# Hybrid encoder layer on one core: 160 columns of the input weights loaded behind the first tile, and the keys' latents projected between the transposes of the input

## The chip, the cores and the metric

The kernel runs on one core of a Trainium2 chip. The metric is the device time of one execution in microseconds (us), the median over several runs. Everything is float32. The engines named below are TensorE (PE, with PEld for its weight loads), VectorE (DVE), ScalarE (ACT), GpSimd (POOL) and SyncE (SP), which here only issues transfers.

## The reference

One encoder layer on a sequence of 512 tokens with 1024 features. The part around the change is the norm and the combined input projection, from which three mixers read their slices:

```python
xn = rms_norm(x, norm1_g[l])
proj = xn @ w_in[l]                      # 1024 x 1472
gq, gk, gv, gg, gaf, gab, fu, cq, ckv, kr = jnp.split(proj, split_at, axis=-1)
o_gla = gla_mixer(gq, gk, gv, gg, gaf, gab, ...)
o_fnet = fnet_mixer(fu, fnet_w[l])
o_mla = mla_mixer(cq, ckv, kr, cos, sin, ...)
x = x + jnp.concatenate([o_gla, o_fnet, o_mla], axis=-1) @ w_out[l]
x = x + hier_moe(rms_norm(x, norm2_g[l]), ...)   # 32 experts, top 2
```

`ckv` (128 columns) is the latent from which the attention's keys and values are made, `kr` (32 columns) the rotary part of the keys. They are the last 160 of the 1472 columns of `w_in`.

## The kernel before

The tokens are four tiles of 128 (`T` = 4), the features eight groups of 128 (`C` = 8). Each engine runs its own instruction list in the order in which the code issues it, and semaphores join them. The eight PSUM banks (512 float32 columns each) are given out by `psum_plan`, a list written by hand: `ring` takes the next bank, `open_bank` lets PE wait until the bank's last reader is through, `filled` lets a reader wait for PE, and `drained` lets anyone wait until the readers are through.

The order at the start is this. SP issues the positions, the four tiles of x (0.5 MB each, semaphores `x_landed`), and then `w_in` in three pieces: columns 0 to 255 (q and k of the linear attention, 1 MB), 768 to 1471 (2.8 MB), 256 to 767 (2 MB). PE transposes x (L747), eight 128x128 blocks for each tile of tokens; the block of group c goes to bank c, so a bank is full only when the last tile has been transposed. ACT (even banks) and DVE (odd banks) copy the eight banks into `xnT`, scaled by the first norm's gain, one instruction of 512 columns for each bank (L1283, L1532). ACT also squares x for the norm (L1275, two instructions in the profile for each tile: the square and the read of its sum), two tiles before and two behind its copies. The norm's root is applied to the products, not to x: DVE builds `rdiag` from it (L1538, semaphore `rstd_ready`).

PE's products follow: `pT 1` (L771, q by feature, waits for the first piece of `w_in` and for each copied bank), `R` (L776), `pT 2` (L755), `pT 0` (L781), then for each tile t the product `ckr` (L763, 160 columns: latent and rotary part of the keys) and the product `ucq` (L763, 512 columns), with the two gate products `z` (L792) behind the first tile's, and then four products `vg` (L763, 512 columns). Each product by token is eight matmuls, one for each group of features; a float32 matmul shows as two records in the profile. Behind them come the latents' transposes (L801, L806, wait for `latents_ready`), those of the gated keys (L812, wait for `gla_ready`), and all of the attention, the output projection, the router and the experts.

ACT copies each `ckr` product to SBUF, squares its latent and then squares a part of `ucq` (`copy_ckr`, L1294 to L1299), in turns with the exponentials of the gates. The experts' weights (3 MB for each of 32 experts) stream through seven places in SBUF; SP issues a load when PE is through with the place's last expert (`gu_full`, L631, `y_full`, L636; for the first place that comes free `gu_half`, L677).

Of the kernel before, what the change touches and what calls it, by code (L numbers as in the profile page):

```python
# [30 lines left out]
ALU = mybir.AluOpType  # L31
# [3 lines left out]
P = 128  # L35
# [33 lines left out]
def psum_plan():  # L69
# [12 lines left out]
    def ring(key, readers=1):  # L82
        use(key, turn[0] % 8, readers)
        turn[0] += 1

    for c in range(C):
        ring(("xT", c))
# [4 lines left out]
    for t in range(T):  # L92
        ring(("ckr", t))
        ring(("ucq", t))
        if t == 0:
            ring(("z", 0))
            ring(("z", 1))
# [134 lines left out]
def encoder_kernel(nc, d, out):  # L232
    ctx = ExitStack()
    with ctx:
# [170 lines left out]
        win_landed = [sem(f"win_landed{i}") for i in range(3)]  # L405
# [164 lines left out]
        def _(sp):  # L570
# [3 lines left out]
            for t in range(T):  # L574
                sp.dma_start(X[:, t, :], x_v[:, t, :]).then_inc(x_landed[t], 16)
            sp.dma_start(w_in_sb[:, :, GQ:GV], w_in_v[:, :, GQ:GV]).then_inc(win_landed[1], 16)
            sp.dma_start(w_in_sb[:, :, GA:W_IN], w_in_v[:, :, GA:W_IN]).then_inc(win_landed[0], 16)
# [161 lines left out]
        def _(pe):  # L739

            pe.wait_ge(ident_landed, 16)
            for t in range(T):
                pe.wait_ge(x_landed[t], 16)
                for c in range(C):
                    if t == 0:
                        open_bank(("xT", c))
                    mm = pe.transpose(banks[PLAN[("xT", c)][0]][:, t * P:(t + 1) * P], X[:, t, c:D:C], ident[:, :])  # L747
                    if t == T - 1:
                        close_bank(mm, ("xT", c))
# [16 lines left out]

            pe.wait_ge(win_landed[1], 16)
            ps = open_bank(("pT", 1))
            for c in range(C):
                drained(pe, ("xT", c))  # L770
                mm = pe.matmul(ps[:, :], w_in_sb[:, c, GQ:GQ + 128], xnT[:, c, :], start=(c == 0), stop=(c == C - 1))  # L771
            close_bank(mm, ("pT", 1))
# [11 lines left out]
            for t in range(T):  # L784
                by_token(("ckr", t), t, CKV, 160)
                by_token(("ucq", t), t, FU, 512)
                if t == 0:
                    pe.wait_ge(gate_w_landed, 16 * 8)
                    drained(pe, ("pT", 0))
                    for dd in range(2):  # L790
                        ps = open_bank(("z", dd))
                        close_bank(pe.matmul(ps[:, :], wa[:, dd, :], gaT[:, :], start=True, stop=True), ("z", dd))  # L792
# [463 lines left out]
        def _(act):  # L1256
# [20 lines left out]

            square_x(0)
            square_x(1)
            act.wait_ge(first_landed, 48)  # L1280
            for c in range(0, C, 2):
                ps = filled(act, ("xT", c))
                free_bank(act.activation(xnT[:, c, :], ps[:, :], ACT.Copy, scale=gain1[:, c:c + 1]), ("xT", c))  # L1283
            square_x(2)
            square_x(3)
            root_guess(stat[:, 8:12], stat[:, 4:8])
# [5 lines left out]
            def copy_ckr(t):  # L1292
# [4 lines left out]
                act.wait_ge(squares_ready, T + 2 * t + 1)  # L1297
                drained(act, ("ucq", t))
                act.activation(squares_out, ucq[:, t, 256:512], ACT.Square, accum_out=stat[:, 16 + t:17 + t]).then_inc(squares_ready, 1)  # L1299
                act.wait_ge(squares_ready, T + 2 * t + 2)  # L1300

            act.wait_ge(rstd_ready, T)
            copy_ckr(0)

# [4 lines left out]
            copy_ckr(1)  # L1309
# [5 lines left out]
            copy_ckr(2)  # L1315
            copy_ckr(3)
# [180 lines left out]
        def _(dve):  # L1497
# [32 lines left out]
            for c in range(1, C, 2):  # L1530
                ps = filled(dve, ("xT", c))
                free_bank(dve.tensor_scalar(xnT[:, c, :], ps[:, :], gain1[:, c:c + 1], None, ALU.mult), ("xT", c))  # L1532
# [573 lines left out]
```

## Time and profile before

| | |
|---|---|
| median of 3 runs | 520.05 us (518.36 to 520.24) |
| the profiled execution's own time | 521.45 us |
| its span on the core | 519.6 us |
| PE busy | 488.5 us (94%) |
| DVE, ACT, POOL busy | 213.0, 137.7, 75.5 us |
| HBM read, written | 129.94 MB, 16.39 MB |

The span is the stretch from the first to the last instruction of the profiled execution; 1.85 us of its time lie around it. PE's busy time counts pipelined matmuls with modelled ends. The profile divides the span into 40 slices of 13 us; the DMA engines are busy at 90% or more in the last 20 slices but one, which is the time of the experts.

### The profile page before, as it was taken

To read this page: it belongs to the slowest core of one execution; us is meant where nothing else is said; L and a number is where in the kernel's file an instruction comes from. 1 tells how busy PE (TensorE), PEld (TensorE's weight loads), DVE (VectorE), ACT (ScalarE), POOL (GpSimd) and SP (SyncE) were. 2 spreads that over 40 slices of the span, in tenths; PEclk is the share of its full clock that TensorE was granted. 3 is DMA by queue.
4 is the path that set the end of the run, shared out by engine and by line. 5 is a ranking of instruction groups with operands and counts; after the bars stand their busy time and mean duration, and the time that the engine had idled before them with its cause. 6 is when DMAs were issued, how large, how long until landed. Compare 5 with 4: busy or idle time off the path is not lost.

```text
span 519.6 us, 7646 instructions
## 1 busy us (share of the span) xinstructions
PE 488.5 (94%) x2904; PEld 262.6 (51%) x2904; DVE 213.0 (41%) x562; ACT 137.7 (27%) x359; POOL 75.5 (15%) x101
## 2 busy tenths in 40 slices
PE   4999999999999999999999899999999998879894
PEld 4446544567655554455455555555555554444431
DVE  3217330576776661116853322222222222242167
ACT  4404211354676661213131111111111111112023
POOL 1000000352100000001122122222222222111000
PEclk9999999999999999999999899999999999999998
DMA  8995000010298005941398999999999999999974
GB/s 299 360 276 223 2 1 0 16 37 3 77 420 354 1 1 211 425 173 42 96 334 301 408 373 422 419 419 418 418 419 418 418 418 419 420 419 420 401 289 162
DMA packets 35543, 139.42 MB, mean 268 GB/s; under 512 B 9865, under 2 KB 11977, under 8 KB 23473
## 3 DMA queue, kind: packets, MB, share of 16 engines
q1 hardware_dynamic: 30160, 130.85, 64.3%
q0 software_dynamic: 4816, 7.85, 4.1%
q8 instruction: 24, 0.39, 0.3%
q10 hardware_dynamic: 528, 0.22, 0.2%
q14 instruction: 15, 0.11, 0.1%
HBM read 129.94 MB, written 16.39 MB: 282 GB/s over the span
## 4 chain that ended last, share of the span: by engine, by line
PE 72%; DMA 17%; DVE 6%; SPq 3%; issue 1%; ACT 1%; DVEq 0%; POOLq 0%; ACTq 0%
PE bank L1090 16%; PE bank L763 12%; PE bank L952 9%; PE bank L1103 7%; DMA MIX<-in_moe_w_up 6%; DMA EW<-in_moe_w_up 5%; PE bank L925 4%; PE bank L997 3%; PE bank L986 3%; DMA EW<-y_scratch 2%; PE bank L1062 2%; DMA EW<-in_w_in 2%; SPq L631 2%; PE bank L771 1%; PE bank L869 1%; DMA y_scratch<-G,sidx 1%
## 5 line engine op out<-in xcount | busy, mean ns | idle before, releaser
L1090 PE MATMUL bank<-EW,WO 128*64 128x256 f32 x640 | 78.5, 397 | 6.9 <-DMA EW<-in_moe_w_up 4.2
L763 PE MATMUL bank<-EW,XT 128*128 128x512 f32 (+1 forms) x192 | 64.1, 495 | 0.0
L1090 PEld LDWEIGHTS bank<-EW,WO 128*64 128x64 f32 x640 | 45.0, 137 | 35.1 <-DMA EW<-in_moe_w_up 6.6
L952 PE MATMUL bank<-WO,XT 128*128 128x512 f32 x128 | 56.9, 596 | 0.0
L1444 ACT ACTIVATE G<-bank 128x128 f32<-128x128 f32 x32 | 8.9, 278 | 179.1 <-PE bank L1090 169.5
L1815 DVE TENSOR_TENSOR G<-G,bank 128x128 f32<-128x128 f32 x32 | 9.2, 288 | 107.4 <-ACT G L1444 107.4
L2040 POOL DMA_INDIRECT y_scratch<-G,sidx x30 | 30.5, 1017 | 154.3 <-DVE G L1828 138.9
L763 PEld LDWEIGHTS bank<-EW,XT 128*128 128x128 f32 x192 | 32.9, 190 | 31.0 <-issue 31.0
L1828 DVE COPY G<-bank 128x512 f32<-128x512 f32 x32 | 22.1, 692 | 46.2 <-PE bank L1103 46.2
L1103 PE MATMUL bank<-EW,G 128*64 128x512 f32 x160 | 38.2, 599 | 0.0
L952 PEld LDWEIGHTS bank<-WO,XT 128*128 128x128 f32 x128 | 23.6, 190 | 26.9 <-issue 26.9
L925 PE MATMUL bank<-EW 96*128 96x512 f32 x64 | 32.8, 596 | 0.9 <-ACT WO L1363 0.6
L1680 DVE TENSOR_REDUCE nm<-bank 128x1 f32<-128x512 f32 x32 | 22.0, 689 | 14.3 <-PE bank L925 14.1
L2034 POOL DMA_INDIRECT list_scratch<-lrow,dest x8 | 7.9, 990 | 131.0 <-DVE dest L1772 129.8
L1374 ACT ACTIVATE G<-bank,nm 128x512 f32<-128x512 f32 x32 | 22.0, 688 | 12.0 <-DVE nm L1680 10.0
L986 PEld LDWEIGHTS bank<-ident,G 128*128 128x128 f32 x128 | 15.3, 140 | 14.9 <-issue 13.9
L1434 ACT ACTIVATE WO<-bank,gain 128x128 f32<-128x128 f32 x64 | 18.3, 369 | 14.2 <-PE bank L1062 14.2
L1394 ACT ACTIVATE EW<-bank 128x512 f32<-128x512 f32 x32 | 18.7, 590 | 8.9 <-PE bank L986 8.9
L986 PE MATMUL bank<-ident,G 128*128 128x128 f32 x128 | 19.3, 275 | 0.0
L1103 PEld LDWEIGHTS bank<-EW,G 128*64 128x64 f32 x160 | 10.4, 135 | 15.6 <-issue 13.2
L1090 PE MATMUL bank<-MIX,WO 128*64 128x256 f32 x128 | 15.4, 391 | 2.1 <-DMA MIX<-in_moe_w_up 2.1
L1090 PE MATMUL bank<-XT,WO 128*64 128x256 f32 x128 | 15.4, 391 | 2.0 <-DMA XT<-in_moe_w_up 2.0
(296 smaller groups left out, 623.5 us busy)
## 6 DMA issues: line engine op xcount, KB each, us to landing
EW<-in_moe_w_down SPq DMA_DIRECT2D x20, 1024.0 KB, 22.4
EW<-in_moe_w_gate SPq DMA_DIRECT2D x19, 1024.0 KB
EW<-in_moe_w_up SPq DMA_DIRECT2D x19, 1024.0 KB
y_scratch<-MIX SPq DMA_DIRECT2D x8, 512.0 KB, 8.4
WO<-in_w_out SPq DMA_DIRECT2D x2, 2048.0 KB, 11.7
MIX<-in_moe_w_gate SPq DMA_DIRECT2D x4, 1024.0 KB
MIX<-in_moe_w_up SPq DMA_DIRECT2D x4, 1024.0 KB
G<-in_moe_w_down SPq DMA_DIRECT2D x4, 1024.0 KB
```

The costliest lines, as they stand in the source:

```text
L763: mm = pe.matmul(ps[:, 0:width], xnT[:, c, t * P:(t + 1) * P], w_in_sb[:, c, col:col + width], start=(c == 0), stop=(c == C - 1))
L925: close_bank(pe.matmul(ps[:, :], qT[0:QD, h, tq * P:(tq + 1) * P], kT[0:QD, h, :], start=True, stop=True), ("S", i))
L952: mm = pe.matmul(ps[:, :], xnT[:, c, t * P:(t + 1) * P], w_out_sb[:, c, n * 512:(n + 1) * 512], start=(c == 0), stop=(c == C - 1))
L986: mm = pe.transpose(ps[:, kc * P:(kc + 1) * P], probs[:, i % 4, kc * P:(kc + 1) * P], ident[:, :])
L1090: mm = pe.matmul(bank[BLOCK * m:BLOCK * (m + 1), 0:2 * P].rearrange("p (w n) -> p w n", w=2), xeT[:, c, par * BLOCK:(par + 1) * BLOCK], wv ...
L1103: mm = pe.matmul(bank[BLOCK * q:BLOCK * (q + 1), :], hT[:, par, m, :], wv[:, m, q * 512:(q + 1) * 512], start=(m == 0), stop=(m == 1))
L1374: free_bank(act.activation(probs[:, i % 4], ps[:, :], ACT.Exp, bias=nm[:, i:i + 1], accum_out=rs[:, i:i + 1]), ("S", i))
L1394: free_bank(act.activation(probsT[:, g, u, :, tile * P:(tile + 1) * P], ps[:, :].rearrange("p (k n) -> p k n", k=T), ACT.Copy), ("PT", j))
L1434: ins = act.activation(xeT[:, c], banks[half][:, j * P:(j + 1) * P], ACT.Copy, scale=gain2[:, c:c + 1])
L1680: dve.tensor_reduce(nm[:, i:i + 1], ps[:, :], AX, ALU.max, negate=True).then_inc(neg_max, 1)
L1828: dve.tensor_copy(Y[:, e % 2], banks[4 + e % 2][:, :]).then_inc(y_ready, 1)
L2040: pool.indirect_dma_start(y_rows, bass.IndirectOffsetOnAxis(ap=sidx[:, col:col + 1], axis=0), Y[:, e % 2], None, bounds_check=4 * S - 1, o ...
```

## The change

The last 160 columns of `w_in` become a transfer of their own, issued behind the first tile of x. The transposes go to two banks for each tile (four groups each), so that a tile can be copied as soon as it has been transposed: DVE copies four groups with one instruction of 512 columns, ACT the other four with four instructions of 128 columns. PE makes the four `ckr` products between and behind the transposes. The other products keep their order. ACT copies all four `ckr` before it squares the first `ucq`. The core of the diff:

```diff
-    for c in range(C):
-        ring(("xT", c))
+    for t in range(T):
+        for q in range(2):
+            ring(("xT", t, q))
+    for t in range(T):
+        ring(("ckr", t))
     ring(("pT", 1))
     ring("R")
     ring(("pT", 2))
     ring(("pT", 0))
     for t in range(T):
-        ring(("ckr", t))
         ring(("ucq", t))
...
             for t in range(T):
                 sp.dma_start(X[:, t, :], x_v[:, t, :]).then_inc(x_landed[t], 16)
+                if t == 0:
+                    sp.dma_start(w_in_sb[:, :, CKV:W_IN], w_in_v[:, :, CKV:W_IN]).then_inc(win_landed[3], 16)
             sp.dma_start(w_in_sb[:, :, GQ:GV], w_in_v[:, :, GQ:GV]).then_inc(win_landed[1], 16)
-            sp.dma_start(w_in_sb[:, :, GA:W_IN], w_in_v[:, :, GA:W_IN]).then_inc(win_landed[0], 16)
+            sp.dma_start(w_in_sb[:, :, GA:CKV], w_in_v[:, :, GA:CKV]).then_inc(win_landed[0], 16)
...
+            def transpose_x(t):
                 pe.wait_ge(x_landed[t], 16)
+                for q in range(2):
+                    ps = open_bank(("xT", t, q))
+                    for j in range(4):
+                        mm = pe.transpose(ps[:, j * P:(j + 1) * P], X[:, t, 4 * q + j:D:C], ident[:, :])
+                    close_bank(mm, ("xT", t, q))
...
+            def key_latent(t):
+                for q in range(2):
+                    drained(pe, ("xT", t, q))
+                by_token(("ckr", t), t, CKV, 160)
+
+            transpose_x(0)
+            pe.wait_ge(win_landed[3], 16)
+            key_latent(0)
+            transpose_x(1)
+            transpose_x(2)
+            key_latent(1)
+            transpose_x(3)
+            key_latent(2)
+            key_latent(3)
             pe.wait_ge(win_landed[1], 16)
-            ps = open_bank(("pT", 1))
-            for c in range(C):
-                drained(pe, ("xT", c))
-                mm = pe.matmul(ps[:, :], w_in_sb[:, c, GQ:GQ + 128], xnT[:, c, :], start=(c == 0), stop=(c == C - 1))
-            close_bank(mm, ("pT", 1))
+            by_feature(("pT", 1), GQ, 128)
...
             for t in range(T):
-                by_token(("ckr", t), t, CKV, 160)
                 by_token(("ucq", t), t, FU, 512)
...
+            def copy_x(t):
+                ps = filled(act, ("xT", t, 1))
+                for j in range(4):
+                    ins = act.activation(xnT[:, 4 + j, t * P:(t + 1) * P], ps[:, j * P:(j + 1) * P], ACT.Copy,
+                                         scale=gain1[:, 4 + j:5 + j])
+                free_bank(ins, ("xT", t, 1))
+
             square_x(0)
+            act.wait_ge(first_landed, 48)
+            copy_x(0)
             square_x(1)
-            act.wait_ge(first_landed, 48)
-            for c in range(0, C, 2):
-                ps = filled(act, ("xT", c))
-                free_bank(act.activation(xnT[:, c, :], ps[:, :], ACT.Copy, scale=gain1[:, c:c + 1]), ("xT", c))
             square_x(2)
+            copy_x(1)
+            copy_x(2)
             square_x(3)
+            copy_x(3)
...
             act.wait_ge(rstd_ready, T)
-            copy_ckr(0)
-
+            for t in range(T):
+                copy_ckr(t)
+            square_cq(0)
...
+            def copy_x(t):
+                ps = filled(dve, ("xT", t, 0))
+                free_bank(dve.tensor_tensor(xnT[:, 0:4, t * P:(t + 1) * P], ps[:, :].rearrange("p (c n) -> p c n", c=4),
+                                            gain1[:, 0:4].unsqueeze(2).to_broadcast([P, 4, P]), ALU.mult), ("xT", t, 0))
+
             dve.wait_ge(first_landed, 48)
+            copy_x(0)
             dve.tensor_copy(lrow[:, :, :, 0], small[:, 41:49].rearrange("p (t r) -> p t r", t=T)).then_inc(row_ready, 1)
```

On PE, at the start of the program, the order before was this. L747 are the transposes, L771 the product `pT 1`, which waits for one copied bank after another (`bank_free`) and for its weights (`win_landed1`):

```order
L747 MATMUL bank<-ident,X 128x128 [waits x_landed0,ident_landed]
L747 MATMUL bank<-ident,X 128x128 x7
L747 MATMUL bank<-ident,X 128x128 [waits x_landed1]
L747 MATMUL bank<-ident,X 128x128 x7
L747 MATMUL bank<-ident,X 128x128 [waits x_landed2]
L747 MATMUL bank<-ident,X 128x128 x7
L747 MATMUL bank<-ident,X 128x128 [waits x_landed3]
L747 MATMUL bank<-ident,X 128x128 x7
L771 MATMUL bank<-XT,EW 128x512 [waits bank_free0,win_landed1]
L771 MATMUL bank<-XT,EW 128x512 [waits bank_free1]
```

The same place on PE in the changed kernel, whose line numbers differ: L751 are the transposes, L766 the `ckr` products:

```order
L751 MATMUL bank<-ident,X 128x128 [waits x_landed0,ident_landed]
L751 MATMUL bank<-ident,X 128x128 x7
L766 MATMUL bank<-EW,XT 128x160 [waits bank_free1,bank_free0,win_landed3]
L766 MATMUL bank<-EW,XT 128x160 x7
L751 MATMUL bank<-ident,X 128x128 [waits x_landed1]
L751 MATMUL bank<-ident,X 128x128 x7
L751 MATMUL bank<-ident,X 128x128 [waits x_landed2]
L751 MATMUL bank<-ident,X 128x128 x7
L766 MATMUL bank<-EW,XT 128x160 [waits bank_free1,bank_free3,bank_free2]
L766 MATMUL bank<-EW,XT 128x160 x7
L751 MATMUL bank<-ident,X 128x128 [waits x_landed3]
L751 MATMUL bank<-ident,X 128x128 x7
```

Behind these rows stand the other two `ckr` products and then `pT 1`, so all four are now ahead of it. The first waits for the copies of the first tile, and the transposes of the other tiles stand behind it.

On ACT, at the start of the program, the order before: L1275 squares, L1283 copies, L1268 begins the norm's root:

```order
L1275 ACTIVATE MIX,stat<-X 128x1024 [waits x_landed0]
L1275 ACTIVATE MIX,stat<-X 128x1024 [waits x_landed1,squares_ready]
L1283 ACTIVATE XT<-bank,gain 128x512 [waits bank_full0,first_landed,squares_ready]
L1283 ACTIVATE XT<-bank,gain 128x512 [waits bank_full2]
L1283 ACTIVATE XT<-bank,gain 128x512 [waits bank_full4]
L1283 ACTIVATE XT<-bank,gain 128x512 [waits bank_full6]
L1275 ACTIVATE MIX,stat<-X 128x1024 [waits x_landed2]
L1275 ACTIVATE MIX,stat<-X 128x1024 [waits x_landed3,squares_ready]
L1268 ACTIVATE stat<-stat 128x4 [waits var_ready,squares_ready]
```

And in the changed kernel, where L1287 squares and L1293 copies:

```order
L1287 ACTIVATE MIX,stat<-X 128x1024 [waits x_landed0]
L1293 ACTIVATE XT<-bank,gain 128x128 [waits bank_full1,first_landed,squares_ready]
L1293 ACTIVATE XT<-bank,gain 128x128 x3
L1287 ACTIVATE MIX,stat<-X 128x1024 [waits x_landed1]
L1287 ACTIVATE MIX,stat<-X 128x1024 [waits x_landed2,squares_ready]
L1293 ACTIVATE XT<-bank,gain 128x128 [waits bank_full3,squares_ready]
L1293 ACTIVATE XT<-bank,gain 128x128 x3
L1293 ACTIVATE XT<-bank,gain 128x128 [waits bank_full5]
L1293 ACTIVATE XT<-bank,gain 128x128 x3
L1287 ACTIVATE MIX,stat<-X 128x1024 [waits x_landed3]
L1293 ACTIVATE XT<-bank,gain 128x128 [waits bank_full7,squares_ready]
L1293 ACTIVATE XT<-bank,gain 128x128 x3
```

Four copies of 512 columns have become sixteen of 128, each tile's copies stand behind a square, and the third square stands ahead of the second tile's copies.

## Rows read from the trace of the kernel before

**Rows 1.** PE's waits over the span: us in total, times, longest.

```profile
PE bank L747 <- DMA X<-in_x: 5.5, 1, 5.5
...
PE bank L1090 <- DVE rslot L1848: 1.9, 1, 1.9
...
PE bank L771 <- DMA EW<-in_w_in: 1.7, 1, 1.7
```

**Rows 2.** The chain that ended last: start, us, what.

```profile
3.46 9.26 DMA EW<-in_w_in
12.76 7.13 PE bank L771 x16
...
40.43 54.59 PE bank L763 x160
...
407.79 32.36 DMA MIX<-in_moe_w_up
```

**Rows 3.** SP's queue, 120 to 330 us, in order of time.

```profile
275.96 0.33 SPq L677 DMA_DIRECT2D EW<-in_moe_w_gate  x1
```

**Rows 4.** Busy by stretch: PE, PEld, DVE, ACT, POOL; then clock, DMA share, GB/s.

```profile
5.40:6.90 1.50, 1.41 (x7) 1.45 (x8) 0.25 (x3) 1.12 (x2) 0.00 (x0) 1.00 1.01 385
...
20.00:30.00 10.00, 10.00 (x38) 4.06 (x37) 2.54 (x4) 0.00 (x0) 0.00 (x0) 1.00 1.10 229
...
320.00:400.00 80.00, 80.00 (x565) 41.18 (x563) 23.37 (x51) 10.47 (x37) 19.04 (x19) 1.00 1.02 419
```

**Rows 5.** PE, 0 to 150 us: start, us, line, operation, count, idle before.

```profile
5.49 5.62 PE L747 MATMUL bank<-ident,X 128*128 128x128 f32 x32 [5.49 <-DMA X<-in_x]
...
29.40 9.31 PE L763 MATMUL bank<-EW,XT 128*128 128x160 f32 x32
...
96.25 1.04 PE L812 MATMUL bank<-ident,WO 128*128 128x128 f32 x8
```

**Rows 6.** PE in the window 8.4 to 8.9 us.

```profile
8.08 1.06 PE L747 MATMUL bank<-ident,X 128*128 128x128 f32 x4
```

**Rows 7.** PE in the window 9.93 to 10.7 us.

```profile
9.71 1.17 PE L747 MATMUL bank<-ident,X 128*128 128x128 f32 x9
```

**Rows 8.** Line L747, the transposes of x at the start: ns min/median/max.

```profile
L747 PE MATMUL bank<-ident,X x32: 272/421/451, 5.5 to 10.8; 128*128 128x128 f32 x32
```

**Rows 9.** Line L1019, the same transpose later: ns min/median/max.

```profile
L1019 PE MATMUL bank<-ident,X x32: 272/274/348, 216.1 to 261.4; 128*128 128x128 f32 x32
```

**Rows 10.** By form, 0 to 96 us: busy us, mean ns, idle before.

```profile
L763 PE MATMUL bank<-EW,XT 128*128 128x160 f32 x64 | 9.5, 301 | 0.0
```

**Rows 11.** All engines, 0 to 48 us, in order of time.

```profile
5.37 1.06 ACT L1275 ACTIVATE MIX<-X 128x1024 f32<-128x1024 f32 x1 [1.85 <-DMA X<-in_x]
...
6.34 0.19 ACT L1275 ACTIVATION_READ_ACCUMULATOR MIX<-X 128x1 f32 x1
6.62 0.17 DVE L1515 COPY lrow<-small 128x8 f32<-128x8 f32 x1 [6.62 <-DMA gain<-in_norm_g]
...
7.12 1.06 ACT L1275 ACTIVATE MIX<-X 128x1024 f32<-128x1024 f32 x1 [0.60 <-DMA X<-in_x]
...
17.95 1.28 ACT L1291 ACT_TABLE_LOAD   x1
...
27.66 0.69 DVE L1546 TENSOR_TENSOR G<-bank,MIX 128x512 f32<-128x512 f32 x1 [5.45 <-PE bank L755]
```

**Rows 12.** ACT in the window 286 to 288 us: four copies of 128 columns.

```profile
286.38 1.14 ACT L1434 ACTIVATE WO<-bank,gain 128x128 f32<-128x128 f32 x4 [2.52 <-PE bank L1062]
```

**Rows 13.** DVE, 47 to 96 us: the last instruction of the gates' chain.

```profile
55.43 0.69 DVE L1584 TENSOR_TENSOR WO<-G,dec 128x512 f32<-128x512 f32 x1
```

**Rows 14.** PE in the window 290 to 310 us, around a long wait.

```profile
295.78 5.44 PE L1090 MATMUL bank<-EW,WO 128*64 128x256 f32 x32 [1.89 <-DVE rslot L1848]
```

**Rows 15.** PE there in quarters of a us: busy; granted clock, DMA share, GB/s.

```profile
296.50:296.75 0.25, 0.25 (x4) 0.50 1.24 524
...
299.75:300.00 0.25, 0.25 (x6) 1.00 0.84 295
```

More of the change, by code:

```diff
@@ L404, in encoder_kernel @@
         x_landed = [sem(f"x_landed{t}") for t in range(T)]
-        win_landed = [sem(f"win_landed{i}") for i in range(3)]
+        win_landed = [sem(f"win_landed{i}") for i in range(4)]
         first_landed = sem("first_landed")
@@ L741, in _ @@
             pe.wait_ge(ident_landed, 16)
-            for t in range(T):
+            def transpose_x(t):
                 pe.wait_ge(x_landed[t], 16)
-                for c in range(C):
[L745 to L749, printed above, removed]
+                for q in range(2):
[3 more added lines that the diff above has]
+                    close_bank(mm, ("xT", t, q))
             def by_feature(key, col, width):
@@ L765, in by_token @@
                 close_bank(mm, key)
-            pe.wait_ge(win_landed[1], 16)
-            ps = open_bank(("pT", 1))
-            for c in range(C):
-                drained(pe, ("xT", c))
-                mm = pe.matmul(ps[:, :], w_in_sb[:, c, GQ:GQ + 128], xnT[:, c, :], start=(c == 0), stop=(c == C - 1))
-            close_bank(mm, ("pT", 1))
+            def key_latent(t):
[11 more added lines that the diff above has]
+            key_latent(3)
+            pe.wait_ge(win_landed[1], 16)
+            by_feature(("pT", 1), GQ, 128)
             pe.wait_ge(ones_ready, 1)
@@ L1296, in copy_ckr, with square_cq @@
                 act.activation(squares_out[:, 0:128], ckr[:, t, 0:128], ACT.Square, accum_out=stat[:, 20 + t:21 + t]).then_inc(squares_ready, 1)
-                act.wait_ge(squares_ready, T + 2 * t + 1)
+                act.wait_ge(squares_ready, T + t + 1)
+            def square_cq(t):
                 drained(act, ("ucq", t))
                 act.activation(squares_out, ucq[:, t, 256:512], ACT.Square, accum_out=stat[:, 16 + t:17 + t]).then_inc(squares_ready, 1)
-                act.wait_ge(squares_ready, T + 2 * t + 2)
+                act.wait_ge(squares_ready, 2 * T + t + 1)
             act.wait_ge(rstd_ready, T)
-            copy_ckr(0)
+            for t in range(T):
+                copy_ckr(t)
+            square_cq(0)
             for dd in range(2):
@@ L1308, in _ @@
                 act.activation(gexp[:, dd, 1], gexp[:, dd, 0], ACT.Ln, bias=1.0).then_inc(gate_log, 1)
-            copy_ckr(1)
+            square_cq(1)
             for dd in range(2):
@@ L1314, in _ @@
                 act.activation(dec[:, dd], tot[:, dd], ACT.Exp, scale=1.0 / TAU).then_inc(decay_exp, 1)
-            copy_ckr(2)
-            copy_ckr(3)
+            square_cq(2)
+            square_cq(3)
             root_guess(stat[:, 32:40], stat[:, 24:32])
@@ L1527, in _ @@
             dve.tensor_scalar(kk, kk, float(np.pi / 2), None, ALU.add).then_inc(angles_ready, 1)
-            for c in range(1, C, 2):
-                ps = filled(dve, ("xT", c))
-                free_bank(dve.tensor_scalar(xnT[:, c, :], ps[:, :], gain1[:, c:c + 1], None, ALU.mult), ("xT", c))
+            for t in range(1, T):
+                copy_x(t)
             dve.wait_ge(squares_ready, T)
```

## The prediction

> **What bounds the kernel now.** I read PE's waits first [rows 1]. PE waits 5.5 us for the first tile of x, 1.7 us for the first piece of `w_in`, and then for nothing until the attention, some 130 us in; only short waits follow until the experts. So up to the experts the time is PE's own work. The chain that ended last [rows 2] says the same: from 12.76 us on it runs on PE from product to product, among them one piece of 54.59 us that holds the last `ckr` products. The late part is another matter. From about 320 us the DMA engines move 419 GB/s without a gap [rows 4], and the chain runs through a transfer of experts' weights of 32.36 us [rows 2]. But that stream begins with issues that PE releases: the first place that comes free is reloaded at 275.96 us [rows 3], behind the first expert's first products. What PE gains or loses before that moves the stream and with it the end, one for one. So I ask one question: when does PE begin the product `pT 1`, once the four `ckr` products are counted on one side in both kernels?
>
> **Before.** `pT 1` begins at 12.76 us [rows 2]. The four `ckr` products come later and cost 9.5 us of PE for 64 records [rows 10], 0.148 us a record or 2.37 us a product. With them moved ahead and nothing else, `pT 1` would begin at 12.76 + 9.5 = 22.26 us. That is the number to beat.
>
> **A clock behind the transposes.** The 32 transposes take 5.62 us [rows 5], and not evenly. In one window four take 1.06 us [rows 6]: less the last one's 0.42 us, the median of the line [rows 8], that is 0.64 / 3 = 0.213 us from one to the next. In a later window nine take 1.17 us [rows 7]: (1.17 - 0.27) / 8 = 0.112 us. The same form takes a median 0.274 us later in the kernel against 0.421 us here [rows 8, 9]. [...] The records grant 1.00 at this time [rows 4], so the level is my reading of the spacing. If n transposes ran slow, 0.213n + 0.112(32 - n) = 5.62 - 0.3 gives n = 17: the clock rose about 5.49 + 17 x 0.213 = 9.1 us, taken as 9.3.
>
> **After, step by step.** Removed: PE's wait of 1.66 us for the first piece of `w_in`, which is far behind its landing when `pT 1` comes. Added, in PE's order:
>
> Tile 0 is transposed from 5.49 us at the slow rate: the last of eight starts at 5.49 + 7 x 0.213 = 6.98 and ends at 7.40. DVE copies its half at about 7.0 to 7.7 us: its bank is full at about 6.6, the gain lands at 6.62 [rows 11], and 512 columns from a bank take 0.69 us, as the form with two operands does [rows 11]. ACT has to square tile 0 first, 5.37 to 6.53 [rows 11], which is over before the second bank is full. Then four copies of 128 columns take 1.14 us [rows 12]: 7.45 to 8.6. So the first `ckr` begins at about 8.65, and PE has a new wait of 1.25 us, with all other transposes behind it.
>
> The weights for it: 655 KB behind the first tile. At 385 GB/s [rows 4] that is 1.7 us, landing at 7.1; at the worst rate of the nearest rows, 229 GB/s [rows 4], 2.9 us and 8.3. Both are ahead of 8.65, so the transfer is hidden behind the copies. The other tiles come 1.7 to 2.9 us later than before: tile 1, squared from 7.12 before [rows 11], at 8.8 to 10.0, and the others 1.36 us apart (524 KB at 385 GB/s), tile 3 at 11.5 to 12.7. All are needed later than that. [...]
>
> First `ckr`: slow until 9.3 (0.3 us a record by the factor of two, so two records), the other 14 at 0.148: ends at about 11.35. Transposes of tiles 1 and 2: 16 x 0.112 = 1.8, to 13.15. Second `ckr`: needs ACT's copies of tile 1. Its bank is full at 12.45; ACT's second and third squares (1.25 us each, 8.8 to 11.4) are done; copies to 13.6. A wait of 0.5 us. It ends at 13.65 + 2.37 = 16.0. Tile 3: to 16.9. Third `ckr` (its copies end at 14.8): to 19.3. ACT's last square takes 14.8 to 16.05, its copies of tile 3 17.1 to 18.3, ahead of the last `ckr`: 19.3 to 21.65. `pT 1` begins at about 21.7.
>
> Sum: 22.26 - 21.7 = 0.55 us earlier. By parts: 1.66 us of waiting gone, 1.75 us of waiting new, 15 - 6 = 9 transposes fewer at the slow rate saves 0.9, two slow records of `ckr` cost 0.3. The sum is made on the profiled execution (521.45 us, span 519.6), 1.4 us above the median of the runs; a shift of half a us is the same on both. 520.05 - 0.55 = 519.5.
>
> **Edits costed at nothing.** The norm's root comes later on ACT, behind the last copies at 18.3, with `rdiag` about 2.1 us after them (root, three small steps, four instructions of 0.22), at 20.4. `R` needs it behind `pT 1` (7.13 us [rows 2]), at 28.8: cover of 8 us. ACT's four `ckr` copies follow the table loads (1.28 us each [rows 11]) at about 22, and no bank of theirs is used again before `ucq 0`, at 21.7 + (29.40 - 12.76) = 38.3 us [rows 5, 2]. The gate products `z` come 3 x 2.37 - 0.55 = 6.6 us later than before, since all four `ckr` are ahead of them and not only one, so their chain on DVE ends at about 63 instead of 56; its reader on PE is at 96.25 [rows 13, 5]. The latents' norm stays where it is, since the last `ucq` moves only by the sum above. Nothing behind `ckr` on SP or POOL waits for a thing that moves: SP only issues 1,024 more short rows in a queue that is full of data anyway. Were these covers gone, the largest would cost the 2.1 us of `rdiag`.
>
> **Rivals.** *The clock stays low through the first `ckr`.* The change cuts the run of transposes by a wait of 1.25 us where before PE ran unbroken. This kernel shows what a wait can do: before L1090 PE waits 1.89 us, the granted clock stands at 0.50 as it resumes and is back at 1.00 at 299.75 [rows 15], and 32 records take 5.44 us [rows 14]. Before, the rise came 9.3 - 5.49 = 3.8 us after PE began. If the wait makes that count anew from the first `ckr`, it comes at 8.65 + 3.8 = 12.5: 13 records run slow instead of two, 11 x 0.15 = 1.7 us more than in my sum. Then 520.05 - 0.55 + 1.7 = 521.2, slower than before. It decides from a rise at about 10.4 us on: from there the gain is gone. Against it: the wait is shorter than 1.89 us, and the wait of 1.66 us before `pT 1` left the clock up. [...]
>
> *More is gained.* If the copies are quick and the clock is up by the first `ckr`, 0.3 us more is saved; and if in runs of before that nobody profiled the wait of 1.66 us brought the clock down (some 3.5 us at half rate, as in [rows 14, 15], are 1.7 us lost), the change saves that too: 518.2.
>
> *The shift is swallowed.* If the experts' stream does not hang on PE, nothing moves: 520.05. Against it stands the issue at 275.96, which waits for PE [rows 3].
>
> *The transfer breaks the order.* If the short rows run at a third of the rate (5 us), tile 1 lands at 12, and PE waits another 1.7 us: 521.2 too. No row has such a rate.
>
> **How the numbers follow.** My forecast 519.5, own range 518.8 to 520.1: 0.45. Clock low, or low for part of it, 521.2: 0.25. More gained, 518.2: 0.12. Swallowed, 520.05: 0.1. Slow transfer, 521.2: 0.03. Something that I do not see, either way: 0.05. Half a per cent is 2.6 us, about what a measurement can tell from no change; no case reaches it alone. Two together, clock and transfer, could. The runs also scatter, from 518.36 to 520.24. The range is 518.0 to 521.9. Faster by over 0.5%: 0.07; within: 0.84; slower: 0.09.
>
> **What would show it.** In the profile of the changed kernel: PE idle of 1.0 to 1.5 us ahead of the first `ckr` (released by ACT's copies, not by the DMA); transposes of tiles 1 to 3 at 0.11 us; a short wait ahead of the second `ckr`, released by ACT; `pT 1` at 21.3 to 22.1 us without a wait for weights; no new wait until 96 us; the first L677 issue as much earlier as `pT 1` is against 22.26. I am wrong if the first `ckr` takes over 3 us, if PE waits for `win_landed3` or a tile, or if `pT 1` begins after 22.5.

## The result and the profile after

The changed kernel takes **521.87 us** (median of 11 runs, 520.60 to 523.91) against 520.05 us (518.36 to 521.34, 11 runs): a ratio of 1.0033, with a 95% interval of 1.0018 to 1.0048. It is slower, by a third of a per cent. Forecast was 519.5 us. The range, 518.0 to 521.9, holds the time at its very edge, but the step was in the other direction.

PE's work in order of time, 0 to 320 us (start, us, line, operation, count, idle before and what ended it):

```profile
5.79 1.94 PE L751 MATMUL bank<-ident,X 128*128 128x128 f32 x8 [5.79 <-DMA X<-in_x]
9.26 3.89 PE L766 MATMUL bank<-EW,XT 128*128 128x160 f32 x16 [1.52 <-ACT XT L1293]
12.98 1.94 PE L751 MATMUL bank<-ident,X 128*128 128x128 f32 x16
15.36 2.41 PE L766 MATMUL bank<-EW,XT 128*128 128x160 f32 x16 [0.44 <-issue]
17.61 1.05 PE L751 MATMUL bank<-ident,X 128*128 128x128 f32 x8
18.49 4.51 PE L766 MATMUL bank<-EW,XT 128*128 128x160 f32 x32
22.84 7.03 PE L758 MATMUL bank<-XT,EW 128*128 128x512 f32 x16
...
97.53 1.04 PE L824 MATMUL bank<-ident,WO 128*128 128x128 f32 x8
...
297.06 3.84 PE L1102 MATMUL bank<-EW,WO 128*64 128x256 f32 x32 [1.89 <-DVE rslot L1876]
```

Compare the rows of one form. Eight transposes take 1.94 us at the first tile, and sixteen take the same 1.94 behind the first `ckr`. Sixteen records of `ckr` take 3.89 us the first time and 2.41 the second. So the first tile's transposes and most of the first `ckr` ran at half rate, and nothing later in these rows did. The trace keeps a list of the clock that TensorE was granted, and it agrees: its first entry, at full clock, begins at 12.28 us, and at 9.40 us in the kernel before. `pT 1` (here L758) begins at 22.84 us.

The chain that ended last, 0 to 60 us (start, us, what), shows what stands ahead of it:

```profile
1.27 4.39 DMA X<-in_x
...
7.86 1.15 ACT XT L1293 x4
9.01 0.25 issue
9.26 3.89 PE bank L766 x16
13.14 1.78 PE bank L751 x16
14.92 0.44 issue
15.36 2.41 PE bank L766 x16
17.77 0.88 PE bank L751 x8
18.66 4.35 PE bank L766 x32
23.00 6.87 PE bank L758 x16
```

PE's waits over the span, and what ended them (total, times, longest; answers to [rows 1]):

```profile
PE bank L751 <- DMA X<-in_x: 5.8, 1, 5.8
...
PE bank L1102 <- DVE rslot L1876: 1.9, 1, 1.9
PE bank L766 <- ACT XT L1293: 1.5, 1, 1.5
```

The wait for `w_in` is gone, and a wait of 1.5 us for ACT's copies has come, ahead of the first `ckr`. The two nearly cancel. What doesn't cancel is the slow `ckr` behind the second.

**Against the kernel before, on one side.** The row of two `ckr` back to back is the cleanest price for one: 4.35 / 2 = 2.18 us (the chain), where I had 9.5 / 4 = 2.37 with modelled ends in it. So before's `pT 1`, with four `ckr` counted ahead, is at 12.76 + 4 x 2.18 = 21.5 us. After is at 22.84, 1.3 us behind. SP's queue, 120 to 330 us, repeats it at the first reload (answers to [rows 3]):

```profile
277.25 0.33 SPq L681 DMA_DIRECT2D EW<-in_moe_w_gate  x1
```

It is 277.25 - 275.96 = 1.29 us later. The first transposes behind the projections, 96.25 us before, stand at 97.53 (1.28). So one shift, made in the first 23 us, is carried through unchanged for 250 us: no wait in between took anything from it or added to it. 1.29 us are 0.25% of the time, and 0.33% (0.18 to 0.48) were measured.

### The profile page after: what moved, and what is told of

Same layout as the page of the kernel before. It is cut to its first block, busy times and chain, and to the rows that moved or that the text cites. A ratio compares the mean times of both kernels' runs of the same rounds, so it can differ in the third digit from the quotient of the medians.

```text
span 520.0 us, 7665 instructions
## 1 busy us (share of the span) xinstructions
PE 487.5 (94%) x2904; PEld 262.1 (50%) x2904; DVE 212.2 (41%) x562; ACT 139.8 (27%) x371; POOL 75.3 (14%) x101
## 4 chain that ended last, share of the span: by engine, by line
PE 74%; DMA 10%; SPq 8%; DVE 6%; issue 1%; ACT 1%; DVEq 0%; POOLq 0%; ACTq 0%
PE bank L1102 15%; PE bank L766 13%; PE bank L964 9%; PE bank L1115 7%; SPq L635 6%; DMA EW<-in_moe_w_up 5%; PE bank L937 4%; PE bank L1009 3%; PE bank L758 3%; PE bank L998 3%; PE bank L1074 2%; DMA EW<-y_scratch 2%; SPq L640 2%; DMA y_scratch<-G,sidx 1%; PE bank L881 1%; PE bank L1245 1%
## 5 line engine op out<-in xcount | busy, mean ns | idle before, releaser
L1102 PE MATMUL bank<-EW,WO 128*64 128x256 f32 x640 | 76.9, 391 | 7.9 <-DMA EW<-in_moe_w_up 5.2
L766 PE MATMUL bank<-EW,XT 128*128 128x512 f32 (+1 forms) x192 | 66.2, 506 | 2.0 <-ACT XT L1293 1.5
L766 PEld LDWEIGHTS bank<-EW,XT 128*128 128x128 f32 x192 | 34.5, 199 | 33.5 <-issue 33.5
L1397 ACT ACTIVATE G<-bank,nm 128x512 f32<-128x512 f32 x32 | 22.0, 688 | 12.2 <-DVE nm L1708 10.0
```

The lines of the kernel that those rows point to most:

```text
L766: mm = pe.matmul(ps[:, 0:width], xnT[:, c, t * P:(t + 1) * P], w_in_sb[:, c, col:col + width], start=(c == 0), stop=(c == C - 1))
L1102: mm = pe.matmul(bank[BLOCK * m:BLOCK * (m + 1), 0:2 * P].rearrange("p (w n) -> p w n", w=2), xeT[:, c, par * BLOCK:(par + 1) * BLOCK], wv ...
L1397: free_bank(act.activation(probs[:, i % 4], ps[:, :], ACT.Exp, bias=nm[:, i:i + 1], accum_out=rs[:, i:i + 1]), ("S", i))
```

## The experiments

Three things were open. **The clock**: does the new wait hold TensorE at half its rate (transposes 0.213 us apart and not 0.112 [rows 6, 7]) through the first `ckr`, and is that the whole loss? **The transfer**: the first tile landed 0.3 us later than before (5.79 against 5.49 us). Is it the new 655 KB behind it that delays it? **The order**: what do tile-wise copies cost by themselves? Where a kernel below adds transposes of the identity, or products of a tile of ones, nothing reads their results; the rest of the computation is unchanged in all of them. A float32 matmul shows as two records, a transpose as one (16 for the eight matmuls of a `ckr`, 8 for the eight transposes of a tile). Each ratio is to the kernel before in runs on the same chip (medians there 520.66, 520.27 and 519.89 us), and is not the quotient of two medians.

**Fill the wait.** The changed kernel with six transposes of the identity between the first tile's transposes and the first `ckr`:

```diff
             transpose_x(0)
+            for _ in range(6):
+                pe.transpose(banks[7][:, 0:P], ident[:, :], ident[:, :])
             pe.wait_ge(win_landed[3], 16)
```

> The changed kernel, with six extra transposes of the identity into a free bank on PE behind the first tile's transposes, where the changed kernel waits 1.52 us; nothing reads them. Theory A (the wait keeps the clock low through the first ckr product): PE's gap shrinks to 0.2 to 0.3 us, the clock rises at about 9 to 10 us, the first ckr takes 2.2 to 2.7 us in place of 3.89, pT 1 begins at 21.2 to 21.8 in place of 22.84, and the whole is 1.0 to 1.6 us faster than the changed kernel: ratio to before 1.0003 to 1.0014. Theory B (the cost lies in the copies' handover and the later tile 0, not in the clock): the first ckr still takes 3.9 us, ratio 1.0033. Theory C (the first ckr is slow because its operands are still being written to or loaded beside the transfers): the same as B.

Measured: 520.72 us, ratio to the kernel before 1.0006 (0.9988 to 1.0024). PE in order of time:

```profile
6.38 1.95 PE L751 MATMUL bank<-ident,X 128*128 128x128 f32 x8 [6.38 <-DMA X<-in_x]
8.12 1.40 PE L777 MATMUL bank<-ident 128*128 128x128 f32 x6
9.85 2.41 PE L766 MATMUL bank<-EW,XT 128*128 128x160 f32 x16 [0.33 <-ACT XT L1295]
...
21.96 7.03 PE L758 MATMUL bank<-XT,EW 128*128 128x512 f32 x16
```

The first `ckr` now takes 2.41 us, as every other. It starts 0.59 us later than in the changed kernel (the tile came later still, at 6.38), and yet `pT 1` starts 0.88 us earlier. Only the idle time ahead of `ckr` was changed, from 1.52 to 0.33 us. The list of the clock begins at 9.30 us here, among the added transposes, and at 12.28 in the changed kernel.

**Early products as well.** On top of it, 18 products of ones while PE waits for the first tile:

```diff
+            pe.wait_ge(ones_ready, 1)
+            for _ in range(18):
+                pe.matmul(banks[7][:, 0:P], ones, ones, start=True, stop=True)
             pe.wait_ge(ident_landed, 16)
```

> As e1, and 18 extra 128x128 products of the ones tile on PE before the first tile of x lands, from about 1.3 us on, so that the clock is up when the work begins. Theory A: the clock has risen by the first tile or soon behind it; the first tile's transposes take down to 1.0 us in place of 1.94, the first ckr 2.2, pT 1 begins at 20.3 to 21.2, 1.6 to 2.5 us earlier than in the changed kernel; ratio to before 0.9985 to 1.0002. Theory B and C: pT 1 within 0.3 us of 22.84 and ratio 1.003.

Measured: 520.05 us, ratio 1.0001 (0.9978 to 1.0023). PE's transposes of the first tile take 1.04 us instead of 1.95, the full rate. But the 18 products are 36 records and last to 7.69 us, so the transposes start at 7.53. `pT 1` is at 22.20 us, the first reload at 276.59. The clock rose at 5.77 us, ahead of the first transpose. But the tile had landed by 5.41, when ACT began to square it: I had put in too much work, and `pT 1` came 1.0 us behind the latest time that I had expected.

**Only the transfer.** The kernel before, with nothing but the 160 columns loaded behind the first tile:

```diff
                 sp.dma_start(X[:, t, :], x_v[:, t, :]).then_inc(x_landed[t], 16)
+                if t == 0:
+                    sp.dma_start(w_in_sb[:, :, CKV:W_IN], w_in_v[:, :, CKV:W_IN]).then_inc(win_landed[3], 16)
...
-            sp.dma_start(w_in_sb[:, :, GA:W_IN], w_in_v[:, :, GA:W_IN]).then_inc(win_landed[0], 16)
+            sp.dma_start(w_in_sb[:, :, GA:CKV], w_in_v[:, :, GA:CKV]).then_inc(win_landed[0], 16)
```

> One part of the change alone: the kernel before with the last 160 columns of w_in as a transfer of their own behind the first tile of x; the order of PE, the copies and the banks as before. If the transfer costs what its bytes do (655 KB at 385 GB/s), the first piece of w_in lands 1.7 to 2.2 us later, PE's wait before pT 1 grows from 1.66 to 3.3 to 4.0 us and the kernel is 1.7 to 2.2 us slower, ratio 1.003 to 1.004; if that long wait brings the clock down as well, up to 1.7 us more, ratio up to 1.0075. If short rows are nearly free, ratio 1.000 to 1.001. Tile 0 should land at 5.66 as in the changed kernel if its delay of 0.3 us comes from this transfer, and at 5.37 if not.

Measured: 522.36 us, ratio 1.0030 (1.0012 to 1.0049). PE in order of time:

```profile
6.01 1.94 PE L749 MATMUL bank<-ident,X 128*128 128x128 f32 x8 [6.01 <-DMA X<-in_x]
9.96 5.39 PE L749 MATMUL bank<-ident,X 128*128 128x128 f32 x24 [2.00 <-DMA X<-in_x]
15.50 7.13 PE L773 MATMUL bank<-XT,EW 128*128 128x512 f32 x16 [0.16 <-DMA EW<-in_w_in]
```

The second tile comes 1.18 MB behind the first, PE waits 2.00 us for it, and then all 24 transposes run at 5.39 / 24 = 0.22 us; the list of the clock begins at 15.53 us. Before, those behind the first 19 ran at 0.11. It is what the changed kernel shows, without a `ckr` or a copy in it: a wait early on, and half the rate behind it. `pT 1` begins at 15.50, 2.74 us later than before. In this order the transfer is exposed; in the changed kernel it is hidden.

**Only the early products.** The kernel before with the 18 products of ones:

> The kernel before with the 18 extra products ahead of the first tile. Theory A: the transposes run at the higher rate from the first or second tile on, but pT 1 waits for its weights until 12.76 either way, so nothing is gained, ratio 0.999 to 1.001; the wait before pT 1 grows to some 2.1 us, and if that is enough to bring the clock down, pT 1 begins slow and the kernel is up to 1.7 us slower, ratio 1.003. If before loses time in the slow transposes (they are on the path after all), ratio below 0.998.

Measured: 520.08 us, ratio 0.9995 (0.9976 to 1.0015). PE in order of time:

```profile
1.29 7.06 PE L743 MATMUL bank<-MIX 128*128 128x128 f32 x36 [1.29 <-POOL MIX L1985]
8.19 3.70 PE L750 MATMUL bank<-ident,X 128*128 128x128 f32 x32
12.87 7.13 PE L774 MATMUL bank<-XT,EW 128*128 128x512 f32 x16 [0.98 <-DMA EW<-in_w_in]
```

All 32 transposes at 0.11 us, 3.70 us together instead of 5.62 [rows 5], and nothing is won: the first piece of `w_in` is what `pT 1` waits for in that order. A faster clock before is worth nothing, since the transfer covers it. After, with `w_in` off the path, each slow record counts in full.

**Swap the halves.** The changed kernel, with ACT copying the first bank of each tile, which is full earlier, and DVE the second:

```diff
-                ps = filled(act, ("xT", t, 1))
+                ps = filled(act, ("xT", t, 0))
...
-                ps = filled(dve, ("xT", t, 0))
+                ps = filled(dve, ("xT", t, 1))
```

> The changed kernel with the two copying engines changed over: ACT, whose four copies of a tile take 1.14 us, gets the bank that is filled first, DVE, with one copy of 0.69 us, the bank that is filled last. If the wait ahead of the first ckr is set by ACT's copies, it shrinks from 1.52 us to 0.7 to 0.9 us and the first ckr begins 0.6 to 0.8 us earlier; the wait of 0.44 us ahead of the second ckr goes. If the shorter wait also lets the clock rise earlier, the first ckr takes under 3 us and pT 1 begins 1.8 to 2.6 us earlier relative to tile 0's landing, ratio to before 0.9995 to 1.001; if the clock stays low all the same, the first ckr takes 3.3 to 3.9 us, pT 1 begins 1.0 to 1.3 us earlier, ratio 1.001 to 1.002. If the handover is not what sets the wait, pT 1 begins as long after tile 0 as in the changed kernel (17.05 us) and the ratio stays at 1.0033.

Measured: 521.84 us, ratio 1.0014 (0.9996 to 1.0032). PE in order of time:

```profile
5.67 1.94 PE L751 MATMUL bank<-ident,X 128*128 128x128 f32 x8 [5.67 <-DMA X<-in_x]
8.67 4.60 PE L766 MATMUL bank<-EW,XT 128*128 128x160 f32 x16 [1.06 <-DVE XT L1539]
13.06 2.21 PE L751 MATMUL bank<-ident,X 128*128 128x128 f32 x16
```

Counted from the first transpose the first `ckr` begins 0.47 us sooner (3.00 against 3.47), and the wait is 1.06 us instead of 1.52. The wait of 0.44 us ahead of the second `ckr` is gone. But the first takes 4.60 us, slower than ever, and even the transposes behind it start slow (2.21 against 1.94); the clock rose at 13.63 us. `pT 1` comes at 22.75, 0.09 before the changed kernel's, where I had expected 1.0 us or more. So a shorter wait alone was no cure here; working through it was.

**Swap, and work through the wait.** The same with ten products of ones ahead and four transposes of the identity in the wait:

> The changed kernel with both costs taken off: the engines changed over as in e5, ten extra products of the ones tile from 1.3 us on and four extra transposes of the identity in the wait. Clock theory and handover theory together: tile 0 is transposed in 1.05 us or little more, the first ckr begins 2.3 to 2.8 us after tile 0 lands (3.47 in the changed kernel) and takes 2.4, pT 1 begins at 19.3 to 20.5, 1.0 to 2.2 us ahead of what before has with the ckr on the same side (12.76 + 8.8 = 21.56). Ratio to before 0.996 to 0.998. If the gain is swallowed by the experts' stream, the first reload of an expert's place comes at 274 to 275 us in place of 275.96 and the ratio is still 1.000.

Measured: 519.16 us, ratio 0.9990 (0.9969 to 1.0010). PE in order of time:

```profile
5.98 1.13 PE L754 MATMUL bank<-ident,X 128*128 128x128 f32 x8
...
8.33 2.41 PE L769 MATMUL bank<-EW,XT 128*128 128x160 f32 x16 [0.79 <-DMA EW<-in_w_in]
...
13.27 2.44 PE L769 MATMUL bank<-EW,XT 128*128 128x160 f32 x16 [0.75 <-ACT XT L1298]
```

The clock rose at 6.12 us, and from the second transpose on everything is at full rate. `pT 1` is at 20.78, 0.3 us behind the latest time that I had expected. Two new bounds come to light. The first `ckr` now waits for its weights, landed at 8.3 us, 2.4 us behind the first tile at 5.9. The second waits for ACT, whose square of the third tile stands ahead of the copies of the second.

**The columns behind the second tile.** The kernel with six transposes in the wait, and the 160 columns issued one tile later:

```diff
-                if t == 0:
+                if t == 1:
```

> As e1 (six extra transposes in the wait), with the 160 columns issued behind the second tile of x instead of the first. If the new transfer, in flight beside tile 0, is what delays tile 0, PE begins at 5.1 to 5.6 us and not at 5.8 to 6.4, and tile 1 lands earlier; the columns land at 8.5 to 9.3, about when the copies are through. pT 1 at 21.0 to 21.6, 0.4 to 0.9 us earlier than e1, ratio to before 0.999 to 1.000. If tile 0's landing only scatters from run to run, the ratio is that of e1, 1.0006.

Measured: 520.77 us, ratio 1.0005 (0.9986 to 1.0024); first `ckr` at 8.98 us, 0.25 us of waiting, for the weights, and 2.79 us long, its first records slow, since the clock rose at 9.75; `pT 1` at 21.45. One tile earlier or later makes no difference that shows.

**The changed kernel again,** on the same chip as the last three, since all hangs on one profile of it:

> The changed kernel once more, unchanged, so that the others have it beside them on the same chip and its clock and landings are seen in a second profiled execution. Ratio to before 1.002 to 1.005. By the clock theory the first ckr takes between 2.4 and 3.9 us, by when the clock rises in this execution; by the theory of the copies alone 3.9 again. Tile 0 lands at 5.4 to 6.4.

Measured: 522.02 us (521.25 to 522.93), ratio 1.0035 (1.0019 to 1.0052). PE in order of time:

```profile
6.10 1.94 PE L751 MATMUL bank<-ident,X 128*128 128x128 f32 x8 [6.10 <-DMA X<-in_x]
9.56 4.13 PE L766 MATMUL bank<-EW,XT 128*128 128x160 f32 x16 [1.52 <-ACT XT L1293]
```

The slow first `ckr` comes again, 4.13 us. The filled kernel with its later load ran 522.02 - 520.77 = 1.25 us faster on this chip.

On the transfer theory: ACT squares the first tile as soon as it is there. With the new transfer right behind the tile, that square begins at 5.30 to 6.27 us in eight profiles (5.68 in the changed kernel); without it at 5.14 (early products alone), 5.37 (before), 5.39 (columns a tile later) and 6.00 (tile-wise copies, below). The two groups overlap, so a delay is not shown; one of some 0.3 us, the distance of their means (5.74 and 5.48), is not excluded either.

**ACT's order as well.** The kernel with swap and work in the wait, nine products of ones instead of ten, and ACT's copies of the second tile ahead of its third square:

```diff
-            for _ in range(10):
+            for _ in range(9):
                 pe.matmul(banks[7][:, 0:P], ones, ones, start=True, stop=True)
...
             square_x(1)
-            square_x(2)
             copy_x(1)
+            square_x(2)
             copy_x(2)
```

> As e6, with nine instead of ten extra products at the start and with ACT's copies of tile 1 ahead of its square of tile 2. The wait ahead of the second ckr (0.75 us in e6, released by ACT's copies behind that square) should fall to 0.1 to 0.5 us; the wait ahead of the first ckr, in e6 0.79 us and released by the landing of the 160 columns, stays. pT 1 begins at 20.0 to 20.6 (20.78 in e6), the first reload of an expert's place at 274.5 to 275.1 us (275.18 in e6, 275.96 before). Ratio to before 0.997 to 0.999, the best of all kernels here; if the end no longer follows that reload one for one, 0.999 to 1.001.

Measured: **517.75 us** (517.03 to 518.56, 6 runs) against 519.89, ratio 0.9964 (0.9951 to 0.9977). PE in order of time, and SP's first reload:

```profile
1.29 4.21 PE L747 MATMUL bank<-MIX 128*128 128x128 f32 x18 [1.29 <-POOL MIX L2015]
5.42 1.51 PE L754 MATMUL bank<-ident,X 128*128 128x128 f32 x8
6.77 0.60 PE L780 MATMUL bank<-ident 128*128 128x128 f32 x4
8.00 2.41 PE L769 MATMUL bank<-EW,XT 128*128 128x160 f32 x16 [0.63 <-ACT XT L1298]
10.24 1.93 PE L754 MATMUL bank<-ident,X 128*128 128x128 f32 x16
12.14 2.44 PE L769 MATMUL bank<-EW,XT 128*128 128x160 f32 x16
...
19.64 7.03 PE L761 MATMUL bank<-XT,EW 128*128 128x512 f32 x16
```

```profile
274.05 0.33 SPq L681 DMA_DIRECT2D EW<-in_moe_w_gate  x1
```

The change's own idea wins once PE is kept at work and the copies are put in another order. Read against the changed kernel's timeline, `pT 1` is 3.20 us earlier: 0.37 for the tile's landing, which is scatter, 0.89 between the first transpose and the first `ckr` (3.47 against 2.58), 1.48 in the first `ckr` (3.72 against 2.24 to the next row), 0.48 from there to the second `ckr`, which no longer waits. The reload is 3.20 us earlier too. Against the kernel with ten products `pT 1` is 1.14 us earlier, and 0.56 of that are the first tile's landing; ACT's order is worth 0.79 (from the sixteen transposes' start to the second `ckr` 1.90 us instead of 2.69). The edit touches this second wait alone. That the first `ckr` no longer waits for its weights comes of their landing, 7.7 us here and 8.3 there.

**Only the tile-wise copies.** The kernel before with two banks for each tile and ACT's and DVE's copies tile by tile, ACT's all ahead of the second square; loads and products in the old order:

> Another part of the change alone: the kernel before, with its transfers and its order of products, but with the transposes into two banks for each tile and the copies tile by tile as in the changed kernel. The copies are ready before the first piece of w_in either way, so pT 1 begins at 12.6 to 12.9 us as before and ratio 0.999 to 1.001. If the sixteen short copies on ACT were a cost of their own, pT 1 would begin later than 13.2 and the ratio be above 1.001.

Measured: 521.26 us, ratio 1.0025 (1.0006 to 1.0044). PE in order of time:

```profile
6.12 5.50 PE L748 MATMUL bank<-ident,X 128*128 128x128 f32 x32 [6.12 <-DMA X<-in_x]
13.26 7.11 PE L773 MATMUL bank<-XT,EW 128*128 128x512 f32 x16 [1.64 <-ACT XT L1283]
```

Here `pT 1` waits not for `w_in`, landed at 12.9 us, but for the last tile's copies, which end at 13.0 us on ACT, and begins 0.50 us later than before; I had expected no change. The first piece of `w_in` itself landed 0.2 us later than before (12.72), so some 0.3 us are the copies'. By themselves they gain nothing. The shift at the reload, 276.43 - 275.96 = 0.47 us or 0.09%, explains a third of the ratio; the rest stays open.

**Shift and ratio.** The first reload of each profile against 275.96 us, as a share of the time, beside the measured ratio:

| kernel | first reload | shift | measured |
|---|---|---|---|
| swap, worked through, ACT's order | 274.05 | -0.37% | -0.36% |
| swap, worked through | 275.18 | -0.15% | -0.10% |
| wait filled, columns a tile later | 275.85 | -0.02% | +0.05% |
| early products alone | 276.08 | +0.02% | -0.05% |
| wait filled | 276.37 | +0.08% | +0.06% |
| tile-wise copies alone | 276.43 | +0.09% | +0.25% |
| wait filled and early products | 276.59 | +0.12% | +0.01% |
| swap | 277.14 | +0.23% | +0.14% |
| changed kernel | 277.25 | +0.25% | +0.33% |
| changed kernel again | 277.77 | +0.35% | +0.35% |
| transfer alone | 278.70 | +0.53% | +0.30% |

One profile stands for each kernel, and each ratio has an interval of about 0.15 to 0.2% to either side. All but the last agree within it. What joins reload and end is these medians and not the profiles: from the first reload to the end of the span the twelve profiled executions take 241.0 to 243.8 us, which scatters as widely as the largest shift. In five of them (before, transfer alone, swap, columns a tile later, tile-wise copies) the clock was at half for 3.41 us, from 296.1 to 298.8 us on, as in [rows 15], and they take 242.5 to 243.8; the other seven take 241.0 to 242.8. Whether that stretch counts at the end, and what brings it about in one kernel and not in another, is open.

## Why the prediction was wrong

**The mechanism was right, the clock was not.** I forecast 0.55 us of gain, and the profile shows 1.3 us of loss at `pT 1`. Of the 1.9 us between, some 1.3 are the first `ckr`, 0.3 the first tile's landing, and 0.3 the longer wait ahead of the first `ckr`. The step that failed is "slow until 9.3 [...] so two records, the other 14 at 0.148". I took the time of the clock's rise from the kernel before, where PE ran unbroken, and kept it for a kernel in which PE waits just before it. The trace has the records of the first `ckr` 0.267 us apart up to 12.05 us and 0.136 us (2.18 / 16) from 12.30 on, so the prediction's factor of two for a slow record, which the transposes before show at 0.213 against 0.112 us, holds for these too. 3.89 - 2.41 = 1.48 us are then 11 slow records where the forecast had two: the clock rose at about 9.26 + 11 x 0.27 = 12.2 us. In the second profile of the kernel it was about 13.0, by the same sum. The trace's list has 12.28 and 13.07 us. For the kernel before it has 9.40, so the 9.3 of the prediction was right where it was read.

**The rival had it.** "The clock stays low through the first `ckr`" gave a rise at 12.5 us by counting anew from the first `ckr`, 13 slow records, and 521.2 us; the rise at 12.28, 11 slow records and 521.87 us were measured. It had 0.25 against the forecast's 0.45. Its two counter-arguments don't hold. "The wait is shorter than 1.89 us" was no reason: 1.06 us did as much. "The wait of 1.66 us before `pT 1` left the clock up" compared unlike places: that wait comes behind some 13 transposes at full rate, and the 16 records of `pT 1` took 7.13 us behind it against 7.03 in the changed kernel, where PE had not waited; this one comes while the clock had not yet risen. The traces speak for the rival's reason: the first `ckr` took 3.89, 4.13 and 4.60 us behind an idle wait, 2.41 to 2.79 behind a filled one. One of its grounds doesn't hold either: the wait before L1090 is not shown to have brought the clock down. PE resumed at 295.78 us with the clock at 1.00, and the list has 0.50 from 296.12 to 299.53. All twelve profiles have this wait, at 1.88 to 1.89 us, and in seven of them, the changed kernel's among them, the clock stayed at 1.00 behind it and the 32 records took 3.84 or 3.85 us.

Does the rise only scatter from one execution to the next? The lists of the clock of all twelve profiles answer that:

| kernel | idle wait ahead of the rise | rise | after PE's first record | after the wait |
|---|---|---|---|---|
| changed | 1.52 us | 12.28 us | 6.5 us | 3.0 us |
| changed, again | 1.52 | 13.07 | 7.0 | 3.5 |
| swap | 1.06 | 13.63 | 8.0 | 5.0 |
| transfer alone | 2.00 | 15.53 | 9.5 | 5.6 |
| the other eight | none over 0.5 | 5.77 to 9.82 | 2.9 to 5.9 | |

It does scatter, by 3 us. But all eight kernels without such a wait rose sooner than all four with one, counted from PE's first record; counted from the end of the wait the four fall among the eight. That is the rival's "count anew".

Point by point:
- *Wait ahead of the first `ckr`*, 1.25 us, released by ACT: 1.52, by ACT. The copies took what I gave them; 0.25 us passed from ACT's last copy (9.01) to PE's first product (9.26), which I had left out. ("15 - 6 = 9" in the sum should be 17 - 8, which is 9 as well.)
- *The transfer hidden*, landing at 7.1 to 8.3 us: right, 7.5 us. That is 1.8 us behind the first tile, some 350 GB/s, near the upper of my two rates. PE waited for it only where little else was left to wait for, with landings at 8.3 and 8.8 us.
- *Transposes of tiles 1 and 2*, 1.8 us: 1.78 by the chain. *Second wait*, 0.5 us: 0.44. The chain calls it "issue" and names no releaser. ACT's second and third squares were done at 11.3 us, its copies of tile 1 began at 14.12, when the bank was full, and the swap alone took this wait away. The square ahead of the copies bound only in the faster kernel, where the third tile landed at 10.8 us.
- *A `ckr`*, 2.37 us: 2.18. It stood on both sides, so only the times on the way were too late by it.
- *`pT 1` at 21.7, wrong if after 22.5*, and *wrong if the first `ckr` takes over 3 us*: 22.84 and 3.89, so both of these marks were hit.
- *Edits costed at nothing*: right. The shift of 1.3 us stands alike at 23, 97 and 277 us.
- *One for one to the end*: it fits ten of the eleven rows of the table, by medians. The pair of profiles does not show it. The reload is 1.29 us later, the span 0.4 us longer (520.0 against 519.6); in between, the product behind the wait for `rslot` takes 3.84 us here against 5.44 [rows 14], which puts PE at 300.90 against 301.22 us.

The idle wait as the cause of the slow first `ckr` is shown, by filling it and by shortening it without filling. That it is the whole loss is shown for the 1.3 us at the reload; the median lost 1.8 us, and the half us that is left can be scatter (the interval begins at 0.9 us). Filled kernels stand at 1.0006, 1.0001 and 1.0005, the changed one at 1.0033 and 1.0035; the intervals still overlap a little, and on the chip that had both, twelve runs of each lie 1.25 us apart in the median. Open are what joins the reload to the end, the excess of the tile-wise copies and the shortfall of the transfer alone.

## What to carry to other kernels

Here PE was on the path from its first instruction, and a handover to another engine that left it idle before its clock had risen cost more than its length: behind 1.06 to 1.52 us of idle time the first `ckr` took 3.89 to 4.60 us instead of 2.41, 1.5 to 2.2 us more. So where a kernel's start looks like this one, price the work behind a new wait at both rates, and put unread products into the wait (with six transposes in it and the columns a tile later the kernel ran 1.25 us faster), and before the first data, as long as they end before the data is there (18 products lasted to 7.69 us where the tile had landed by 5.41). Read the rise from the trace's list of the clock or from the spacing of the records. A clock's rise read in one order of work must not be kept for another (9.40 us before, 12.28 and 13.07 in the changed kernel); and a gain that a transfer covers before (the early products alone) can be a real one after.

## What was not expected of the hardware

- The profile's windows grant 1.00 in every one of these starts, at half rate too, unlike at [rows 15]. The list behind them has no entry before the rise, and time without an entry counts as full clock; in ten of the twelve profiles its first entry begins where the spacing of PE's records halves (before: 0.213 us apart up to 9.36 us, an entry from 9.40 on, 0.110 us apart from 9.49 on). In the other two it comes behind the last slow record, at 9.30 behind 9.19 us (wait filled) and at 15.53 behind 14.92 us (transfer alone). PE in the changed kernel, in three windows (us; PE, PEld, DVE, ACT and POOL busy, with their counts; clock, DMA share, GB/s):

```profile
8.50:9.50 1.00, 0.24 (x1) 0.28 (x2) 0.86 (x5) 1.00 (x3) 0.00 (x0) 1.00 1.00 406
9.50:12.00 2.50, 2.50 (x10) 2.50 (x11) 0.70 (x4) 1.69 (x4) 0.00 (x0) 1.00 1.04 394
12.00:14.00 2.00, 2.00 (x17) 2.00 (x17) 0.38 (x1) 0.00 (x0) 0.00 (x0) 1.00 1.10 356
```

  Ten records in 2.50 us and then seventeen in 2.00, both at "1.00"; the first entry begins at 12.28.
- The shortest of the idle waits, 1.06 us, went with a later rise, 13.63 us, than the two of 1.52. It lies within the scatter of the table above; what sets the time within it is open.
- Transposes alone were enough for the rise at 9.40 us: before, nothing else had run on PE when their spacing went from 0.213 to 0.112 us.
- 655 KB in rows of 640 bytes landed 1.8 to 3.0 us behind the first tile in the eight profiles that have them there, about 220 to 360 GB/s, around the bounds of 229 and 385 [rows 4] and not at a third of the rate.
